# Mix product and plain up-projection tiles by halves of the sequence, second norm beside them, eighth mix tile last in the first two sums

## The reference

```
h = rmsnorm(x, norm_mix);  proj = h @ w_in + b_in          # 5 * 1024 columns
A = silu(layernorm(causal_dwconv31(val * sigmoid(gate)))) @ conv_w_out
B = per-group pooled means @ pool_w * pool_scale
x1 = x + (sigmoid(gate_a) * A + sigmoid(gate_b) * B) @ mix_w_out     # the mix product
h2 = rmsnorm(x1, norm_ffn)                                           # the second norm
u = h2 @ ffn_w_up (1024 x 5632);  u = causal_dwconv3(u) + bias;  a, g = split(u)
x = x1 + (gelu(a) * g) @ ffn_w_down (2816 x 1024);  out = rmsnorm(x, norm_final)
```

## Time and profile before

| | |
|---|---|
| three runs | 1385.93 us median (1385.70 to 1386.27) |
| the profiled execution, its own time | 1384.93 us |
| its span in the trace | 1382.7 us |
| PE busy | 1344.4 us, 97% |
| DVE, ACT, POOL busy | 832.7, 400.4, 699.4 us |
| weight transfers `raw<-in_wstream` | 60 of 512 KB |
| granted PE clock, mean | 0.989 |

### The profile page before, as it was taken

One profiled execution on the slowest core, in us unless ns is written; L12 is line 12 of the kernel. 1 busy time (PEld: TensorE's weight loads), 2 busy tenths in 40 slices (PEclk: granted clock), 3 DMA queues, 4 the chain that ended last, 5 costly groups with the idle time before them and its releaser, 6 DMA issues.

```text
span 1382.7 us, 15712 instructions
## 1 busy us (share of the span) xinstructions
PE 1344.4 (97%) x6120; PEld 1117.9 (81%) x6120; DVE 832.7 (60%) x817; ACT 400.4 (29%) x560; POOL 699.4 (51%) x470
## 2 busy tenths in 40 slices
PE   7999999999999999999998999999999998999997
PEld 6888888888888878878776888888888887888887
DVE  7799999999997355512594554445554453311224
ACT  4311221211114440011244444444444433322210
POOL 5645536453453333324378777777777614434101
PEclk9999999999999999999999999999999999999998
DMA  5211011111111112232202222212222237531003
GB/s 191 63 60 46 31 46 46 46 46 46 46 46 46 47 46 98 85 107 91 91 31 92 92 91 77 91 65 89 92 76 91 92 110 285 199 107 62 0 0 122
DMA packets 30768, 110.25 MB, mean 80 GB/s; under 512 B 2800, under 2 KB 8944, under 8 KB 26608
## 3 DMA queue, kind: packets, MB, share of 16 engines
q1 hardware_dynamic: 28176, 99.92, 20.7%
q10 hardware_dynamic: 2528, 9.44, 1.9%
HBM read 89.43 MB, written 19.92 MB: 79 GB/s over the span
## 4 chain that ended last, share of the span: by engine, by line
PE 89%; DVE 4%; DMA 2%; issue 1%; ACT 1%; POOL 0%; POOLq 0%; SPq 0%; DVEq 0%; ACTq 0%
PE ps L1245 29%; PE ps L1247 29%; PE ps L1246 29%; DMA tmp<-g_kept 1%; DVE h_lo L1055 1%; DVE tmp L1041 1%; DVE ga_r L1136 0%; PE ps L1309 0%; PE ps L1299 0%; DVE raw L1117 0%; PE ps L1332 0%; DVE res L1067 0%; DMA g_kept<-raw 0%; DVE res L1222 0%; DVE cv L1032 0%
## 5 line engine op out<-in xcount | busy, mean ns | idle before, releaser
L1245 PE MATMUL ps<-h_lo,w_hi 128*128 128x512 f32 (+1 forms) x1004 | 389.2, 388 | 12.4 <-DVE h_lo L904 7.2
L1246 PE MATMUL ps<-h_hi,w_lo 128*128 128x512 f32 (+1 forms) x1004 | 385.4, 384 | 0.0
L1247 PE MATMUL ps<-h_hi,w_hi 128*128 128x512 f32 (+1 forms) x1004 | 385.3, 384 | 0.0
L987 DVE SCALAR_TENSOR_TENSOR ps<-tmp,par,ps 128x1024 f32<-128x1024 f32 x224 | 267.7, 1281 | 0.0
L439 POOL TENSOR_SCALAR w_hi<-raw 128x1024 fp32r<-128x1024 f32 x60 | 67.9, 1131 | 351.6 <-issue 279.6
L1245 PEld LDWEIGHTS ps<-h_lo,w_hi 128*128 128x128 f32 x1004 | 190.1, 189 | 53.2 <-DVE h_lo L904 8.6
L1246 PEld LDWEIGHTS ps<-h_hi,w_lo 128*128 128x128 f32 x1004 | 190.1, 189 | 37.5 <-issue 0.7
L1247 PEld LDWEIGHTS ps<-h_hi,w_hi 128*128 128x128 f32 x1004 | 189.9, 189 | 37.0
L1245 PE MATMUL ps<-ga_r,w_hi 128*128 128x512 f32 (+1 forms) x428 | 167.2, 391 | 11.9 <-issue 5.3
L1247 PE MATMUL ps<-cv_r,w_hi 128*128 128x512 f32 (+1 forms) x428 | 166.6, 389 | 0.0
L1246 PE MATMUL ps<-cv_r,w_lo 128*128 128x512 f32 (+1 forms) x428 | 166.5, 389 | 0.0
(11 more groups left out here) (182 smaller groups left out, 1812.2 us busy)
## 6 DMA issues: line engine op xcount, KB each, us to landing
raw<-in_wstream SPq DMA_DIRECT2D x60, 512.0 KB, 3.5
tmp<-in_wffn SPq DMA_DIRECT2D x16, 1024.0 KB, 4.9
tmp<-g_kept SPq DMA_DIRECT2D x22, 512.0 KB, 3.7
res<-in_wffn SPq DMA_DIRECT2D x10, 1024.0 KB, 4.9
g_kept<-res SPq DMA_DIRECT2D x14, 512.0 KB, 2.6
raw<-in_wffn SPq DMA_DIRECT2D x5, 1024.0 KB, 4.9
res<-in_xT ACTq DMA_DIRECT2D x4, 1024.0 KB, 4.9
g_kept<-raw SPq DMA_DIRECT2D x8, 512.0 KB, 2.6
```

Of the source, the lines that this page charges most:

```text
L987: dve.scalar_tensor_tensor(out=tile(cv, c) if last else acc, in0=glu(c, t), scalar=w, in1=acc, op0=ALU.mult, op1=ALU.add).then_inc(conv_la ...
L1245: nc.tensor.matmul(out, a_hi, b_lo, start=start, stop=False, skip_group_check=onto)
L1246: nc.tensor.matmul(out, a_lo, b_hi, start=False, stop=False, skip_group_check=onto)
L1247: return nc.tensor.matmul(out, a_hi, b_hi, start=False, stop=stop, skip_group_check=onto)
```

## The change

The mix product becomes 16 jobs of 24 matmuls (all 8 tiles of the first half of the sequence, then all 8 of the second) and the plain up-projection 8 jobs. Each job has a chunk of its own: the same weights are streamed and split a second time for the second half, 12 chunks more. The first two mix jobs do their tiles 0 to 6 first and both eighth tiles last. x1, squares and sums go by halves. The first half is normed beside mix jobs 9 to 12 (`NORM2_AT`), the second half beside the first up-projection jobs. `keep_busy` is gone. POOL's low parts are put between its splits.

```
-N_FFN = N_MIX + KT
-NCHUNKS = N_FFN + 2 * PLAIN
+N_FFN = N_MIX + 2 * KT
+N_UP = 2 * PLAIN
+NCHUNKS = N_FFN + 2 * N_UP
...
+        NORM2_AT = {KT + 1: (0, 1, 2), KT + 2: (3, 4), KT + 3: (5, 6), KT + 4: (7,)}
...   POOL
-            splits(LOOSE, N_FFN // 2 + 1)
-
-            for h in range(2):
-                low_halves(n2[h], *span(h), None)
-            splits(N_FFN // 2 + 1, NCHUNKS // 2)
+            FIRST_LOW = N_MIX + 12
+            splits(LOOSE, FIRST_LOW // 2)
+            lows = {FIRST_LOW + i: (0, (2 * i + 1,)) for i in range(4)}
+            lows |= {N_FFN + 3: (1, (1, 3)), N_FFN + 4: (1, (5, 7))}
+            for n in range(FIRST_LOW, NCHUNKS):
+                split(n, n % 2, n // 2)
+                if n in lows:
+                    h, ks = lows[n]
+                    low_halves(n2[h], *span(h), None, ks)
...   ACT
+            for t in range(KT + 1):
+                x1_square(t)
+            deviation(n2[0], 32, slot(3, *span(0)))
+            for t in range(KT + 1, 2 * KT):
+                x1_square(t)
+                for k in NORM2_AT.get(t, ()):
+                    norm2_high(0, k)
+            deviation(n2[1], 40, slot(3, *span(1)))
+            for k in range(KT):
+                norm2_high(1, k)
...
-            act.wait_ge(w_split, N_FFN + 3)
-            first_a(0, (w_used, N_FFN + 1))
+            act.wait_ge(w_split, NCHUNKS - 1)
+            first_a(0, (w_used, N_FFN + N_UP + 1))
             t_high("T1", 1, four(res, 0, 0))
-            act.wait_ge(w_split, N_FFN + 4)
-            first_b(0, (w_used, N_FFN + 2))
+            act.wait_ge(w_split, NCHUNKS)
+            first_b(0, (w_used, N_FFN + N_UP + 2))
...   DVE
+            def x1_add(t):
+                h, m = divmod(t, KT)
+                half = tile(res, m, *span(h))
+                dve.wait_ge(w_used, N_MIX + t + 1)
+                dve.tensor_tensor(half, bank(t % 4), half, ALU.add).then_inc(x1_done, 1)
...
+            for t in range(KT):
+                x1_add(t)
+                if t:
+                    add_square2(t - 1)
+            add_square2(KT - 1)
+            x1_add(KT)
+            add_square2(KT)
+            invert(n2[0], 32, diag[:, 0:HALF])
+            for t in range(KT + 1, 2 * KT):
+                x1_add(t)
+                add_square2(t)
+                for k in NORM2_AT.get(t, ()):
+                    norm2(0, k)
+            invert(n2[1], 40, diag[:, HALF:SEQ])
+            for k in range(KT):
+                norm2(1, k)
...   PE
-            variance2(0)
-            keep_busy(6)
-            broadcast2(0)
-            variance2(1)
-            keep_busy(8)
...
+            for ks in (range(KT - 1), (KT - 1,)):
+                for t in range(2):
+                    mix(t, ks)
+            for t in range(2, 2 * KT):
+                mix(t, range(KT))
+                if t == KT:
+                    variance2(0)
+                if t == KT + 1:
+                    broadcast2(0)
...
+            for h in range(2):
+                for j in range(N_UP):
+                    pe.wait_ge(*up_free[h][j])
+                    between = {(0, 0): {4: lambda: variance2(1)}, (0, 1): {4: lambda: broadcast2(1)}}.get((h, j), {})
+                    half_job(N_FFN + N_UP * h + j, slot(j, *span(h)), h, range(KT), h_hi, h_lo, low_of(n2[h], True), between)
```

More of the change, by code:

```diff
@@ L194, in build, with sq2 @@
         diag = tmp[:, 0:SEQ]
+        def sq2(t):
+            return sq[1][:, t % 2 * HALF:(t % 2 + 1) * HALF]
+        NORM2_AT = {KT + 1: (0, 1, 2), KT + 2: (3, 4), KT + 3: (5, 6), KT + 4: (7,)}
         raw_ffn = [tmp[:, 0:BLOCK], res[:, 0:BLOCK]]
@@ L297, in build @@
         co_a, co_m, co_hi, co_lo = sems("co_a", "co_m", "co_hi", "co_lo")
-        x1_done, mix_half = sems("x1_done", "mix_half")
+        x1_done = sem("x1_done")
         n2_sq, n2_sum = sems("n2_sq", "n2_sum")
@@ L472, in _, with low_halves @@
                 split(n, n, 0)
-            def low_halves(z, a, b, bufs):
-                for k in range(1, KT, 2):
+            def low_halves(z, a, b, bufs, ks=range(1, KT, 2)):
+                for k in ks:
                     pool.wait_ge(z["hi"], k + 1)
@@ L521, in _ @@
                 if p == PLAIN:
-                    pool.wait_ge(n2_sum, KT + 1)
+                    pool.wait_ge(n2_sum, 2 * KT)
                     pool.wait_ge(gb_done, KT)
@@ L715, in _, with x1_square, norm2_high @@
             kept = x1_kept.rearrange("(k p) n -> p k n", p=P)
[L716 to L733, removed]
+            def x1_square(t):
+                h, m = divmod(t, KT)
+                half = tile(res, m, *span(h))
+                act.wait_ge(x1_done, t + 1)
+                wait(act, n2_sum, t - 1)
+                act.activation(sq2(t), half, ACT.Square).then_inc(n2_sq, 1)
+                act.dma_start(kept[:, m, h * HALF:(h + 1) * HALF], half).then_inc(x1_last if h else x1_loaded, 16)
+            def norm2_high(h, k):
+                act.wait_ge(n2[h]["val"], k + 1)
+                act.activation(tile(h_hi, k, *span(h)), tile(res, k, *span(h)), ACT.Copy).then_inc(n2[h]["hi"], 1)
+            for t in range(KT + 1):
[8 more added lines that the diff above has]
+                norm2_high(1, k)
             def t_high(name, n_sum, src):
@@ L818, in next_high @@
                         down_high(j)
-                first_a(q, (f_post, posted(q, "c12")) if q >= PLAIN else (w_used, N_FFN + 3))
+                first_a(q, (f_post, posted(q, "c12")) if q >= PLAIN else (w_used, N_FFN + N_UP + 3))
                 if q < PLAIN:
-                    first_b(q, (w_used, N_FFN + 4))
+                    first_b(q, (w_used, N_FFN + N_UP + 4))
                 next_high(0)
@@ L1072, in _ @@
             dve.wait_ge(xre_loaded, 16 * (KT // 2))
[L1073 to L1083, removed]
-                else:
[L1085 to L1095, removed]
+            def x1_add(t):
+                h, m = divmod(t, KT)
+                half = tile(res, m, *span(h))
+                dve.wait_ge(w_used, N_MIX + t + 1)
+                dve.tensor_tensor(half, bank(t % 4), half, ALU.add).then_inc(x1_done, 1)
@@ new lines, in add_square2, with norm2 @@
+            def add_square2(t):
+                h, m = divmod(t, KT)
+                a, b = span(h)
+                dve.wait_ge(n2_sq, t + 1)
+                if m == 0:
+                    dve.tensor_copy(csum[:, a:b], sq2(t)).then_inc(n2_sum, 1)
+                else:
+                    dve.wait_ge(n2_sum, t)
+                    dve.tensor_tensor(csum[:, a:b], csum[:, a:b], sq2(t), ALU.add).then_inc(n2_sum, 1)
+            def norm2(h, k):
+                z, half = n2[h], tile(res, k, *span(h))
+                if k == 0:
+                    dve.wait_ge(bc_done, z["nth"])
+                    dve.wait_ge(x1_last if h else x1_loaded, 16 * KT)
+                dve.scalar_tensor_tensor(out=half, in0=half, scalar=par1("norm_ffn", k), in1=slot(2, *span(h)),
+                                         op0=ALU.mult, op1=ALU.mult).then_inc(z["val"], 1)
+                if k % 2:
+                    dve.wait_ge(z["hi"], k)
+                    dve.tensor_tensor(tile(h_lo, k - 1, *span(h)), tile(res, k - 1, *span(h)),
+                                      tile(h_hi, k - 1, *span(h)).bitcast(f32), ALU.subtract).then_inc(z["lo_v"], 1)
@@ L1417, in _ @@
             pairs(N_OUT, ((val_out, KT), (s1_out, out_of(TURN["b", KT - 1]))), co_a, h_hi, h_lo, lambda h, k: (z_lo, h * KT + k + 1))
-            pairs(N_MIX, ((co_a, KT - 1), (co_a, KT)), x1_done, cv_r, ga_r, lambda h, k: (co_lo, k + 1), mix_half)
             def variance2(h):
-                variance(slot(3, *span(h)), [((n2_sum, KT + h), csum[:, h * HALF:(h + 1) * HALF])], var_done)
+                variance(slot(3, *span(h)), [((n2_sum, KT * (h + 1)), csum[:, h * HALF:(h + 1) * HALF])], var_done)
@@ L1423, in broadcast2, with half_job @@
             def broadcast2(h):
                 broadcast(n2[h], slot(2, *span(h)), diag[:, h * HALF:(h + 1) * HALF])
-            variance2(0)
-            keep_busy(6)
-            broadcast2(0)
-            variance2(1)
-            keep_busy(8)
+            def half_job(n, out, h, ks, mov_hi, mov_lo, ready, between={}):
+                pe.wait_ge(w_split, n + 1)
+                for k in ks:
+                    if k in between:
+                        between[k]()
+                    if ready:
+                        pe.wait_ge(*ready(k))
+                    c = n % 2 * CH + k * P
+                    last = three(out, w_hi[:, c:c + P], w_lo[:, c:c + P], tile(mov_hi, k, *span(h)),
+                                 tile(mov_lo, k, *span(h)), k == 0, k == KT - 1)
+                if KT - 1 in ks:
+                    last.then_inc(w_used, 1)
@@ new lines, in mix @@
+            def mix(t, ks):
+                if 0 in ks:
+                    pe.wait_ge(*((co_a, KT - 1) if t < 2 else (co_a, KT) if t < 4 else (x1_done, t - 3)))
```

(13 more changed lines are left out.)

## The result

The changed kernel takes 1393.64 us in the median of five runs (1392.48 to 1394.98), the kernel before 1385.93 (1385.70 to 1388.06): 1.0051 times as long, 95% interval 1.004 to 1.0063. That is 7.7 us slower; 6.0 and 1391.9 were forecast, in the range of 1383.5 to 1396. The profiled execution took 1392.48, 7.6 more than the one before, with a span of 1390.7, 8.0 longer than before.

What follows compares the result with a forecast made beforehand. PE, busy 97% of the span, was taken as bound, with P7 moving the end. 6.7 us gained by the up-projection's start are given back by late t sums and one more split: P7 +6.0, 1385.93 + 6.0 = 1391.9, range 1383.5 to 1396.

Steps and rivals of the forecast that it cites:

- The mechanism: Up-projection to P7: POOL's splits and DVE's sums take turns, with three splits instead of two; P7 at 754.1 against 748.08.
- three waits that were forecast for the splits: Late up-projection: PE wants three splits at S+29.4, 37.7 and 45.3 and waits 2.8, 2.1 and 2.1 us.
- The mix start: First mix jobs: the eighth-tile loss of 2.8 us goes, a 3.25 us third-chunk wait comes; loss 5.0 against 4.5.
- the up-projection starts at 680.2: End of mix: the plain up-projection starts at 680.2 against 686.86, 6.7 us gained; this time is called S.
- The 1.7 us of slow clock: Behind the third-chunk wait at job 2: the same slow clock as before, costing 1.7 us.
- the waits of 0.55 and 0.7: End of mix: slack used up by job 14, so PE waits 0.55 us before job 15 and 0.7 before the up-projection.
- 6.1 us per job on POOL: Mix jobs 12 to 15: split, low part and waits take about 6.1 us per job against 5.44 of matmuls.
- the bounds: Effects listed outside the sum: shared-turn waits, a 1.9 us variance stall, mix waits of 0 or 2.5, late transfers 0 to 1.
- the third rival: More waits: variance stall, late transfers and slow clock in the up-projection, 4 to 6 us more, 1396 to 1398; chance 0.08.
- variance2(1) stalls PE 1.9: First up-projection jobs: if the last half tile's sum of squares comes behind a w_lo, PE stalls 1.9 us.
- S+26.7: S is the up-projection's start; POOL's last rests end 26.7 us later, at 706.9, and DVE's t sums wait for them.
- The faster rival: PE stays the bound, splits and sums fit under matmuls: P7 at 737.4, 10.7 us less, 1375; chance 0.13 with partial forms.

Runs made afterwards that it cites:

- the experiment: The changed kernel with the second half's variance ahead of the eighth instead of the fifth tile of the first up-projection job; 1391.12 us, 1.0033 to the kernel before.
- two chunks shared: Mix by halves with 14 chunks, the first two serving both halves; four-chunk up-projection of the kernel before, second half's variance later; 1375.67 us, 0.9922 to the kernel before.
- up-projection as before: The changed kernel's mix by halves with 16 chunks, but the kernel before's four-chunk plain up-projection and a later second-half variance; 1380.63 us, 0.9957 to the kernel before.
- the last kernel: Mix by halves with 14 chunks, first two serving both halves, four-chunk up-projection, but tiles in order in the first two sums; 1382.09 us, 0.9964 to the kernel before.

## Why the prediction was right

**The mechanism was right.** Slower, because POOL's splits and DVE's t sums take turns and one split more stands behind their start: the t sums began at 707.47 (706.9 forecast), P1 at 736.09 (the turns, summed up to its low part, give 736.1), L551 ended at 746.37 (746.6), P7 began at 753.87 (754.1). From the start of the t sums to the end of L551 the sum of turns, built from durations of the old trace, is 39.7 us, and 38.9 were measured. Experiments bear it out one by one: taking the sums out of the turns gives 7.3 us back, taking half of the transfers gives 0.00, taking the four splits gives 9.2. One of the three waits that were forecast for the splits (2.8, 2.1 and 2.1) did not show: they are 2.13, none and 1.69. Behind the first one PE ran with a slow clock (granted 0.83 in 712 to 722), needed that much longer for the job, and the next chunk was ready about when the job ended (it starts at 720.26, L450 ended at 720.16). With the eighth tile in place no slow clock came there (1.00 in 712 to 722), and the three waits are 2.13, 1.74 and 1.70. P7 is not moved by it, since POOL sets it. The rule of the Trainium skill (SBUF — State Buffer, "Who interferes with whom") that the shared port pair is held for a whole instruction agrees with the rows at 708.35, 710.49 and 712.69.

**The mix start was right.** A wait of 3.15 in place of 2.63, from the third chunk (3.25 forecast); putting the tiles in order moved the time by nothing that can be measured.

**Two terms were mis-sized and met by accident.** "So the up-projection starts at 680.2": it started at 677.60. The 1.7 us of slow clock behind the wait at 599.5 did not come (granted 1.00 in 599.5 to 605 here, 0.76 in 595 to 600 before), and the waits of 0.55 and 0.7 before job 15 and the up-projection did not come either. I had 6.1 us per job on POOL; the rows of POOL say 5.6, because DVE's half tile sum waits behind w_lo and holds up only the short L487, by 0.5:

```profile
661.63 1.47 POOL L448 TENSOR_SCALAR w_hi<-raw 128x1024 fp32r<-128x1024 f32 x1
663.18 2.41 POOL L450 TENSOR_TENSOR w_lo<-raw,w_hi 128x1024 fp32r<-128x1024 f32 x1
665.54 1.75 POOL L487 TENSOR_TENSOR h_lo<-res,h_hi 128x512 fp32r<-128x512 f32 x1
667.26 1.50 POOL L448 TENSOR_SCALAR w_hi<-raw 128x1024 fp32r<-128x1024 f32 x1
```

Those 2.6 us less were met by one that I had put among the bounds and into the third rival: "variance2(1) stalls PE 1.9". It did, by 1.58 and a slow clock, 3.45 in all by the experiment. In the forecast's own terms the t sums should have begun at S+26.7, and began at S+29.9. So 6.0 forecast for P7 against 5.7 measured is a better figure than its parts deserve.

**What the sum did not hold.** P7 is 5.7 us late, the span 8.0 longer. The stretch behind P7 took 634.6 us before (1382.7 - 748.08) and 636.8 in the changed kernel. Nearly all of it is slow clock behind two waits, the one at P7 and one 411 to 412 us later, in code that the change leaves alone. The rows of the kernel before, then those of the changed one:

```profile
748.08:758.08 10.00, 10.00 (x38) 8.19 (x39) 4.19 (x5) 2.94 (x5) 8.64 (x7) 0.85 0.13 52
...
1159.21 0.47 PE L1245 MATMUL ps<-ga_r,w_hi 128*128 128x512 f32 x1 [3.93 <-DVE ga_r L1136]
...
1159.21:1169.21 10.00, 10.00 (x37) 8.11 (x38) 3.21 (x2) 2.16 (x4) 5.03 (x3) 0.83 0.77 255
```

```profile
753.87:763.87 10.00, 10.00 (x35) 8.10 (x36) 3.98 (x4) 2.84 (x4) 8.53 (x7) 0.77 0.14 55
...
1166.18 0.77 PE L1284 MATMUL ps<-ga_r,w_hi 128*128 128x512 f32 x1 [4.36 <-DVE ga_r L1175]
...
1166.18:1176.18 10.00, 10.00 (x33) 8.06 (x34) 3.96 (x3) 3.75 (x6) 5.21 (x4) 0.74 0.73 262
```

0.8 us are the slower clock behind P7: from P7's start to DVE's subtraction behind P4 (L1168 before, L1207 now) it is 9.85 us before and 10.62 now. 0.4 is the second wait itself, 4.36 against 3.93; why it is longer stays open. The last 1.0 lies behind it, where the granted clock of the next 10 us is 0.74 against 0.83, which is 0.9 us of lost work. The seven experiments have the same pattern: the stretch behind P7 takes 635.2 us with granted clocks of 0.85 and 0.83 behind the two waits (two chunks shared), 635.8 with 0.84 and 0.77 (up-projection as before), and 636.8 to 637.2 with 0.74 to 0.77 and 0.72 to 0.74 in the other five. The forecast took the stretch behind P7 as unchanged, and this term it had at nothing.

**The faster rival** (PE stays the bound, P7 10.7 us earlier) was wrong for this kernel and right for its parts: in the last but one kernel, with the splits taken away at the up-projection and the wait at the third chunk, P7 is 10.4 us earlier.

## What to carry to other kernels

Using weights for half as long doubles the work of whoever prepares them: before a product is cut in halves, set the preparing engine's time per chunk, with its worst turns, against the halved matmul time, at each place and not over the span. Where two engines take turns, add up their instructions in the order in which they will stand; the sum is a hard bound, and it moves with one instruction that comes 0.1 us too late. A gain that depends on something being ready (the eighth tile last) is worth testing with the next thing that could be waited for taken away.

## What the runs showed of the hardware that I had not expected

Equal idle stretches of PE at the same place ended differently. 2.63 us at the eighth tile came with a granted clock of 0.72 in the 6 us behind it both in the kernel before and in the last kernel, but of 1.00 in the changed kernel with the eighth tile in place. 3.13 to 3.15 us at the third chunk came with 1.00 in all five kernels that have it, while 1.58 us at 680.5 came with 0.86 in 677.6 to 690 and with a slow clock in all four kernels that have it. 2.13 us at the first of the late splits came with 0.83 in the changed kernel and 1.00 with the eighth tile in place. The clock has two levels, 2.4 GHz and 1.2: in the slow stretch from 714.0 on, matmuls of 512 columns start 0.43 us apart, otherwise 0.227. The length of a gap alone did not decide it here. The slow clock behind the eighth tile cost 1.7 us in the kernel before, so a wait of 2 to 3 us is to be priced with 0 to 1.7 us behind it. The Trainium skill says that the windows in which the chip counts activity run freely beside the kernel (TensorE: Matmul & The Clock Gate, "What's actually happening"); that would let equal gaps end differently, but no run here tests it.
